# A fused pair of hybrid layers on one core: the order of the second block's branches rewritten

## The reference

```
hx = modulate(rmsnorm(x, norm1_g), mod_x[0], mod_x[1])          # 256 tokens x 1024
zx = hx @ w_in                                                  # Hyena 768 | HGRN2 5 x 512 | Fourier 256
# HGRN2 branch: q, forget fwd, forget bwd, v, g; four heads of 128
s_f, s_b, o_c = hgrn2_bidir(context...)                         # states of the context
_, _, o_x = hgrn2_bidir(q_x, v_x, dirs_x, s_f, s_b)             # gated linear attention, both ways
y_hg = o_x * rsqrt(mean(o_x^2)) * hg_norm_g * silu(g_x)
# Hyena branch: short convolution of 3 taps, then two long convolutions by Fourier transform
v, x1, x2 = split(short_conv3(z))
y = x1 * bidir_fftconv(v, h0, h1);  y = x2 * bidir_fftconv(y, h2, h3);  y_hy = rmsnorm(y)
# Fourier branch
y_fn = rmsnorm(real(fft2(z_fn)) @ w + b)
x = x + mod_x[2] * (concat([y_hy, y_hg, y_fn]) @ w_out)
ff = moe_ffn(modulate(rmsnorm(x, norm2_g)))                     # router, 16 experts of 512, top 2
out = rmsnorm(x + mod_x[5] * ff, final_norm_g)
```

## Time and profile before

| | |
|---|---|
| three runs, median | 1199.16 us |
| the profiled execution, its own time | 1197.87 us |
| its span, first to last instruction | 1196.0 us |
| TensorE busy | 1038.1 us, 87% |
| VectorE busy | 567.4 us, 47% |
| ScalarE busy | 395.7 us, 33% |
| GpSimd busy | 46.5 us, 4% |
| mean granted TensorE clock | 0.927 of full speed |
| the stretch from the last q2 matmul to the second tile of out2 | 668.8 to 826.3 us |

### The profile page before, as it was taken

How to read it: one execution, slowest core, us unless ns; L and a number is a source line. 1 busy time by engine, 2 the same in 40 slices (tenths; PEclk the granted TensorE clock), 3 DMA queues, 4 the chain that set the end, 5 groups by cost and what they waited for, 6 DMA issues and landing times.

```text
span 1196.0 us, 13332 instructions
## 1 busy us (share of the span) xinstructions
PE 1038.1 (87%) x5422; PEld 758.2 (63%) x5422; DVE 567.4 (47%) x1031; ACT 395.7 (33%) x664; POOL 46.5 (4%) x66
## 2 busy tenths in 40 slices
PE   5989897797879799989989995837788999999984
PEld 3465785564459689859967694736776565366531
DVE  2363324754345464515542167285584341277815
ACT  2222342643136454314351100212463230256501
POOL 1000000000000000000000022000000000000001
PEclk9999897899789899999989997978789999999988
DMA  9623163046971474356224213000187999799994
GB/s 303 185 93 107 47 224 129 1 141 229 387 298 71 141 253 158 140 198 208 71 94 141 95 48 140 1 1 1 58 333 301 325 349 387 291 404 409 408 388 158
DMA packets 110347, 230.63 MB, mean 193 GB/s; under 512 B 8236, under 2 KB 15693, under 8 KB 110286
## 3 DMA queue, kind: packets, MB, share of 16 engines
q1 hardware_dynamic: 104080, 216.44, 49.9%
q0 software_dynamic: 2880, 9.71, 2.1%
q10 hardware_dynamic: 3326, 3.63, 1.0%
HBM read 221.11 MB, written 8.65 MB: 192 GB/s over the span
## 4 chain that ended last, share of the span: by engine, by line
PE 72%; DVE 13%; DMA 8%; ACT 4%; issue 2%; POOL 0%; ACTq 0%; DVEq 0%; SPq 0%; POOLq 0%
PE bank L637 16%; PE bank L618 8%; PE bank L2398 5%; PE bank L1334 4%; PE bank L1335 4%; PE bank L1336 4%; PE bank L2337 4%; PE bank L2338 4%; PE bank L2339 4%; PE bank L2422 3%; DMA slot<-in_ada_w 3%; DMA more_slots<-in_moe_w_up 2%; DMA slot<-in_w_in 2%; PE bank L2330 2%; PE bank L1377 2%
## 5 line engine op out<-in xcount | busy, mean ns | idle before, releaser
L637 PE MATMUL bank<-x_and_h,slot 128*128 128x256 f32 x768 | 178.5, 390 | 4.9 <-ACT x_and_h L546 4.9
L637 PEld LDWEIGHTS bank<-x_and_h,slot 128*128 128x128 f32 x768 | 147.7, 195 | 32.2 <-issue 9.9
L1335 PE MATMUL bank<-rounded 128*128 128x256 f32 x480 | 136.2, 284 | 0.0
L1334 PE MATMUL bank<-rounded 128*128 128x256 f32 x416 | 121.5, 292 | 4.0 <-DVE slot_rounded L1324 4.0
L618 PE MATMUL bank<-slot,x_and_h 128*128 128x512 f32 x224 | 99.3, 601 | 4.5 <-DVE x_and_h L583 4.5
L1335 PEld LDWEIGHTS bank<-rounded 128*128 128x128 f32 x480 | 91.8, 191 | 0.3
L1336 PE MATMUL bank<-rounded,slot_rounded 128*128 128x256 f32 x296 | 84.3, 285 | 0.0
L1334 PEld LDWEIGHTS bank<-rounded 128*128 128x128 f32 x416 | 79.7, 192 | 6.3 <-issue 5.5
L1324 DVE TENSOR_TENSOR slot_rounded<-slot,rounded 128x1024 fp32r<-128x1024 f32 (+1 forms) x53 | 55.1, 1061 | 58.2 <-ACT rounded L1318 57.9
L618 PEld LDWEIGHTS bank<-slot,x_and_h 128*128 128x128 f32 x224 | 42.8, 193 | 56.1 <-issue 55.1
L647 ACT ACTIVATE arena<-bank 128x256 f32<-128x256 f32 x56 | 21.5, 385 | 145.3 <-PE bank L637 145.2
(11 more groups left out here) (485 smaller groups left out, 2027.4 us busy)
## 6 DMA issues: line engine op xcount, KB each, us to landing
slot<-in_w_in SPq DMA_DIRECT2D x27, 2048.0 KB, 8.3
slot<-in_ada_w SPq DMA_DIRECT2D x12, 2048.0 KB, 12.7
slot<-in_moe_w_down SPq DMA_DIRECT2D x11, 2048.0 KB, 16.4
more_slots<-in_moe_w_gate SPq DMA_DIRECT2D x8, 2048.0 KB, 16.1
more_slots<-in_moe_w_up SPq DMA_DIRECT2D x8, 2048.0 KB, 18.2
slot<-in_moe_w_gate SPq DMA_DIRECT2D x7, 2048.0 KB, 10.2
x_and_h<-in_moe_w_up SPq DMA_DIRECT2D x6, 2048.0 KB, 15.8
more_slots<-in_moe_w_down SPq DMA_DIRECT2D x5, 2048.0 KB, 17.2
```

What stands on the lines that cost most here:

```text
L637: mm = t.do.matmul(bank[:, 0:S], w[:, k, i * P:(i + 1) * P], h[:, k, :], start=k == 0, stop=k == KT - 1)
L1334: t.do.matmul(dst, w_hi, x_hi, start=start, stop=False)
L1335: t.do.matmul(dst, w_hi, x_lo, start=False, stop=False)
```

## The change

The list of jobs from hg_start to the split of cat is written out by hand. The three Hyena branches' jobs start first: hy0's tiles stand around hg_start and the diagonal, convolutions between the levels' sets, the first Hyena round among levels 0 to 2, the second among levels 3 and 4. The set of a level stands some jobs ahead of its products, v2 comes behind level 4's and 5's products, the Fourier jobs around levels 6 and 7, and g2 last, behind hg_close in the list. `out2_start` moves ahead of the last set; the three `cat_split` stand behind g2's second tile (hy, fn) and at the end (hg).

Three edits go with it. `cat_high` gets a home in the arena, at the words of KF (the transformed filters), in place of hT, because g2 still reads hT; ScalarE therefore waits for the second round's products with KF. The memset of the edges of z_hy, which GpSimd did in its queue at convolution 0, moves to hg_start. And each tile of out2 adds up hy and fn before hg, instead of fn, hg, hy.

```diff
-        cat_low, cat_high = tiles_r(0, KT), hT_r
+        cat_low, cat_high = tiles_r(0, KT), tiles_r(3 * KT * S, KT)
...
-        PLAN += woven([("hg_start",), ("hg_diagonal",), *[job for level in range(LEVELS + 1) for job in
-                                          (("hg_set", level), ("hg_scores", level))], ("hg_last_set",)],
-                      [*tokens("v2"), *channels("g2"), *channels("hy0"), *channels("hy1", 2), *[("hy_conv", j) for j in range(6)],
-                       *channels("fn", 2), ("fourier_in", 0), ("fourier_in", 1), ("fourier_turn",), ("fourier_out",)])
-        PLAN += [("hy_tokens", 0), ("hg_out", 0), ("hy_tokens", 1), ("hg_out", 1),
-                 ("hy_freq", 0, 0), ("hg_norm", 0), ("hy_freq", 0, 1), ("hg_norm", 1), ("hy_time", 0), ("norm2", "fn"),
-                 ("hy_freq", 1, 0), ("hg_close",), ("hy_freq", 1, 1), ("hy_time", 1), ("norm2", "hy")]
+        hy0, hy1, v2, fn, g2 = channels("hy0"), channels("hy1", 2), tokens("v2"), channels("fn", 2), channels("g2")
+        PLAN += [hy0[0], ("hg_start",), hy0[1], ("hy_conv", 0), ("hg_diagonal",), hy0[2], ("hg_set", 0), ("hy_conv", 1), ("hg_set", 1),
...
+                 ("hg_out", 0), ("norm2", "hy"), ("fourier_out",), ("hg_out", 1), ("hg_norm", 0), ("hg_norm", 1), ("norm2", "fn"),
+                 ("hg_close",), g2[0], g2[1], ("cat_split", "hy"), ("cat_split", "fn"), g2[2], g2[3], ("cat_split", "hg")]
...
-        @part(GPSIMD, "hy_conv")
-        def gpsimd_hy_conv(g, j):
-            if j == 0:
-                g.wait_ge(*at("response", 1, 1))
-                g.wait_ge(*at("taps_summed", 1, 1))
-                for c in (0, S + 1):
-                    g.do.memset(z_hy[:, :, c:c + 1], 0.0).then_inc(*inc("hy_edges"))
+        @part(GPSIMD, "hg_start")
+        def gpsimd_hy_edges(g):
+            g.wait_ge(*at("response", 1, 1))
+            g.wait_ge(*at("taps_summed", 1, 1))
+            for c in (0, S + 1):
+                g.do.memset(z_hy[:, :, c:c + 1], 0.0).then_inc(*inc("hy_edges"))
...
-            a.wait_ge(*at("channels", "fn", 1))
+            a.wait_ge(*at("hy_products", 1, 1))
...
-            for n, k in enumerate((6, 7, 2, 3, 4, 5, 0, 1)):
+            for n, k in enumerate((0, 1, 6, 7, 2, 3, 4, 5)):
```

9 lines of the change are left out of this document (5 added, 4 removed).

## The result

| | before | after |
|---|---|---|
| median of four runs | 1198.68 us | 1155.13 us (1154.80 to 1155.57) |
| the profiled execution, its own time | 1197.87 us | 1155.06 us |
| its span | 1196.0 us | 1153.3 us |

The ratio is 0.9636, 95% interval 0.9624 to 0.9648: 43.6 us faster. The forecast was 1153.4 us, 1149 to 1161. From profile to profile it is 42.8 us, where 44.5 were forecast. The changed kernel ran a second time later, at a median of 1153.00 us: the two medians of one kernel lie 2.1 us apart.

A forecast was written before the change was run, and what follows sets the result against it. Bound: TensorE's 42.8 us idle and lower clock in the 157.5 us stretch, caused by job order. Stretch 107.4 + 3.9 + 0.4 = 111.7, gain 45.8; 1197.87 - 45.8 + 1.3 = 1153.4 us, range 1149 to 1161.

The forecast's parts named there:

- TensorE's work, 107.4 us: Rewritten stretch, q projection's end to out2's second tile: TensorE's unchanged work at full clock, where 157.5 us passed before.
- The waits 8.27, 6.02 and 19.55 go: TensorE's waits before level 6's and 7's products and the second Hyena inverse transform vanish in the new order.
- The holds by GpSimd: VectorE instructions with two arena inputs held while GpSimd's multiplies run; TensorE waits 1.6 to 5.6 us, 3.9 taken.
- my bound by it was 13.7: VectorE's loss in us over eight levels if every instruction with two arena inputs is held to GpSimd's end.
- the bounds: With everything held, TensorE waits 1.0 us before hy_tokens 0, 2.8 before hy_tokens 1, 5.6 in all.
- 3.9 + 0.4: TensorE waits left in the stretch: 3.9 us with GpSimd's interference, 0.4 for out2's second tile's split weights.
- the first rival: GpSimd's port use holds every two-input VectorE instruction throughout: waits 5.6 us, time 1155.1 us; chance 0.25.
- I cost no lower clock: Rewritten stretch: a wait of 2.8 us was judged nearer to 1.42 than 6.02, so no lower-clock time added.
- The hand-off, level to 1 us: Before out2: VectorE's closing chain, 17.2 us, lies beside 17.3 us of TensorE work including g2.
- the checks named: No TensorE wait over 3 us and clock 1.00 from 669 to 780; GpSimd done by 741; out2's second tile near 780.5.
- The table load, +1.3: New ScalarE table load of 1.28 us before the router's root, all on the experts' chain; bounds 0.5 to 1.3.
- All of it moves up unchanged: out2's last matmul, router and experts keep their order, so everything behind the stretch simply starts earlier.

The follow-up runs named there:

- the outlier of 1195.35 us: One of ten runs of the kernel before with only hg_close moved behind the second Hyena inverse transform; that kernel's median 1202.59 us.
- The five kernels with tails of 341.5 us and more: Kernel before: hg_close moved alone (1202.6 us). Changed kernel: g2 among levels (1170.4), second Hyena turn later (1154.1), Fourier ended earlier (1156.6), root's table loaded early (1156.2).
- the early table: Changed kernel plus one reciprocal root on ScalarE behind the split of cat's hg part, loading that table ahead of the router's root: 1156.15 us.
- three edits that each did what they should: Each alone on the changed kernel: second Hyena turn one tile later (1154.11 us), Fourier branch ended earlier (1156.59), reciprocal root's table loaded early (1156.15).
- a shift of 1.1 us: Changed kernel with the root's table loaded early plus five one-element copies (1.14 us) in front of the router's root: 1154.02 us.

## Why the prediction was right, and where it was off

- TensorE's work, 107.4 us: right. 114.1 less 3.1 of waits, 1.8 in hy1's tile and 1.6 in out2's (4.44 for 2.8) is 107.6.
- The waits 8.27, 6.02 and 19.55 go: right, each is 0. Sets ahead of copies (7.7 us of the stretch) and g2 beside the close (14.2) were each shown by taking them back. That the second Hyena round comes earlier, which the prediction credits with the 19.55, has no run that takes it back alone.
- The holds by GpSimd: right in kind, that tensor_tensor is held too included. The rule drawn from the Trainium skill (SBUF — State Buffer, "SBUF: two separate sides") agrees with the trace here: 10.6 us held in instructions with two inputs from arena, none in the copies; my bound by it was 13.7. The waits were 0.43 and 2.15 us before the turns, where the bounds had 1.0 and 2.8 for them. In all 3.1 us of waits for 3.9 + 0.4. The measured 1155.1 is also the number of the first rival (port held throughout, 5.6 us of waits); that is chance, since its waits did not come, and 10.6 us of holds are below its 13.7.
- "I cost no lower clock" is the step that failed. Behind the 2.15 us it cost 1.8, behind the 0.53 another 1.6 against the forecast's 2.8 for the tile, 0.8 net. I had ranked waits by length, between 1.42 us without and 6.02 with it. Length doesn't decide: 0.53 us was followed by the lower clock and 1.42 was not.
- The hand-off, level to 1 us: right, 0.53. Of the checks named, no wait over 3 us and GpSimd's last pair near 741 (741.6) held. A granted clock of 1.00 did not: it is 0.86 from 706 to 718, though 0.97 over the stretch. Out2's second tile at 780.5 did not either: it starts at 784.98, 2.1 for the front and 2.4 for the clock and the rest.
- The table load, +1.3: right, 31.1 less 29.8.
- "All of it moves up unchanged": wrong by 2.5 us, in the favourable direction. The tail's order kept, but its clock did not: 1.00 behind the wait before L2408, where the kernel before has 0.54 in the first 3.4 us, which is 1.4 of the 2.5 us. Another 1.0 arises some 20 us behind the Exp, where a stretch of 4 us has 0.98 after and 0.68 before.

Stretch 2.4 short, front 2.1 late, tail 2.5 early, table 0.2 less: 44.5 - 2.4 - 2.1 + 2.5 + 0.2 = 42.7, which is the difference of the spans (1196.0 less 1153.3). Part of the nearness to 1153.4 is thus luck: what was missed in the rewritten part and ahead of it, 4.5 us, met 2.5 us in the tail that nobody had forecast.

Open is what the clock goes by, and the outlier of 1195.35 us, which has no trace; its mean granted clock is 0.931, where the other nine runs of that kernel have 0.916 to 0.923. The five kernels with tails of 341.5 us and more all wait 5.2 us instead of some 3.5 for the last weights and lose 1.1 to 1.3 us behind it against the changed kernel; in the trace of the early table the longer wait follows from the clock ahead of it.

## What to carry to other kernels

When queues are in order, ask of each producer what stands ahead of it on every engine, the one that you are not looking at included; and give a closing chain work to lie beside rather than moving it. Before a small edit is called useless or harmful by its total time, cut the trace at fixed events: three edits that each did what they should (5.0, 1.4 and 1.3 us) showed as +1.1, +3.6 and +3.2 us in the total, for stretches at the lower clock far behind them, which a shift of 1.1 us could take away again. Differences of up to 5 us here say something about an edit only once the tails agree.
